# Expert rows loaded over the raw weights, summed, normed and multiplied tile by tile in one block

## What is computed

```python
for layer in range(2):
    h = rmsnorm(x, norm_mix[layer])
    ...
    x = x + mix                       # layer 1: mix = sgu_mixer(h, w_in [1024 x 4096], ...)
    x = x + memory_xattn(rmsnorm(x, norm_xattn[layer]), ...)
    x = x + moe_ffn(rmsnorm(x, norm_ffn[layer]), ...)   # 16 experts, top 2 for each position
```

## Time and profile before

| | |
|---|---|
| median of 3 runs | 1797.41 us (1796.53 to 1797.42) |
| profiled execution, its own time | 1796.38 us |
| its span, first to last instruction | 1794.6 us |
| instructions | 19043 |
| TensorE (PE) matmul busy | 84% of the span |
| VectorE (DVE), ScalarE (ACT), GpSimd (POOL) busy | 50%, 39%, 8% |
| granted TensorE clock, mean | 0.917 of full speed |
| HBM read and written | 267 and 25 MB |

### The profile page before, as it was taken

One profiled execution on the slowest core, in us unless ns is written; L12 is line 12 of the kernel. 1 busy time (PEld: TensorE's weight loads), 2 busy tenths in 40 slices (PEclk: granted clock), 3 DMA queues, 4 the chain that ended last, 5 costly groups with the idle time before them and its releaser, 6 DMA issues. The chain is left out here.

```text
span 1794.6 us, 19043 instructions
## 1 busy us (share of the span) xinstructions
PE 1514.5 (84%) x7481; PEld 1207.5 (67%) x7481; DVE 892.7 (50%) x1247; ACT 707.3 (39%) x1105; POOL 150.6 (8%) x172
## 2 busy tenths in 40 slices
PE   5689698879999893899995699797988894999992
PEld 4577566667777472888883588676877473888872
DVE  3156547575544525566653422743244435666653
ACT  3221355375333412555542333432133432555540
POOL 1000011200000000111101000503000000111110
PEclk9899789989999997899998799898999995999996
DMA  6523021023422053799983242213211133899964
GB/s 181 83 73 97 2 96 48 1 94 118 170 80 71 1 213 135 252 353 362 349 313 144 83 152 94 70 47 132 94 67 51 38 152 143 304 356 355 353 240 182
DMA packets 106874, 275.96 MB, mean 154 GB/s; under 512 B 37649, under 2 KB 40098, under 8 KB 101922
## 3 DMA queue, kind: packets, MB, share of 16 engines
q1 hardware_dynamic: 70818, 203.16, 32.1%
q10 hardware_dynamic: 26464, 54.79, 9.1%
q0 software_dynamic: 9504, 16.80, 2.5%
HBM read 267.31 MB, written 25.17 MB: 163 GB/s over the span
## 5 line engine op out<-in xcount | busy, mean ns | idle before, releaser
L185 DVE TENSOR_TENSOR w_lo<-w_stage,w_hi 128x2048 fp32r<-128x2048 f32 (+2 forms) x48 | 112.0, 2345 | 308.3 <-ACT w_hi L175 291.3
L175 ACT ACTIVATE w_hi<-w_stage 128x2048 fp32r<-128x2048 f32 (+2 forms) x48 | 86.4, 1812 | 338.1 <-PE bank L234 220.6
L2634 PE MATMUL bank<-e_wo,e_actT 128*128 128x512 f32 x384 | 170.4, 593 | 3.5 <-ACT e_actT L2696 3.5
L2517 DVE TENSOR_TENSOR e_wi_lo<-e_wi,w_hi 128x1536 fp32r<-128x1536 f32 x60 | 105.5, 1758 | 78.5 <-ACT w_hi L2513 78.5
L2634 PEld LDWEIGHTS bank<-e_wo,e_actT 128*128 128x128 f32 x384 | 72.2, 190 | 80.8 <-issue 78.9
L2513 ACT ACTIVATE w_hi<-e_wi 128x1536 fp32r<-128x1536 f32 x60 | 89.4, 1489 | 74.2 <-PE bank L2623 47.1
L2517 DVE TENSOR_TENSOR e_wi_lo<-e_wi,w_lo 128x1536 fp32r<-128x1536 f32 x60 | 105.5, 1758 | 16.5 <-ACT w_lo L2513 16.3
L2513 ACT ACTIVATE w_lo<-e_wi 128x1536 fp32r<-128x1536 f32 x60 | 89.0, 1483 | 17.2 <-PE bank L2623 17.2
L2623 PE MATMUL bank<-e_wi_lo,e_hx_hi 128*128 128x384 f32 x256 | 87.1, 340 | 0.0
L2622 PE MATMUL bank<-e_wi_lo,e_hx_hi 128*128 128x384 f32 x256 | 87.0, 340 | 0.0
L193 ACT ACTIVATE w_hi<-w_stage 128x2048 fp32r<-128x2048 f32 x26 | 49.6, 1912 | 85.1 <-PE bank L234 62.1
(11 more groups left out here) (490 smaller groups left out, 3840.9 us busy)
## 6 DMA issues: line engine op xcount, KB each, us to landing
e_wi<-in_moe_w_in SPq DMA_DIRECT2D x128, 768.0 KB, 6.0
e_wo<-in_moe_w_out ACTq DMA_DIRECT2D x30, 1536.0 KB, 9.4
w_stage<-in_x_wkv SPq DMA_DIRECT2D x16, 1024.0 KB, 5.2
w_stage<-in_sg_w_in SPq DMA_DIRECT2D x16, 1024.0 KB, 5.4
w_stage<-in_hyb_w_in SPq DMA_DIRECT2D x10, 1024.0 KB, 5.3
w_stage<-in_x_wq SPq DMA_DIRECT2D x8, 1024.0 KB, 5.0
w_stage<-in_x_wo SPq DMA_DIRECT2D x8, 1024.0 KB, 5.9
w_stage<-in_sg_w_out SPq DMA_DIRECT2D x8, 1024.0 KB, 5.0
```

The lines of the kernel that those rows point to most:

```text
L175: act.activation(self.w_hi[h][:, :, :cols], self.stage[h][:, :, :cols], ACT.Copy)\
L185: dve.tensor_tensor(self.w_lo[h][:, :, :cols], self.stage[h][:, :, :cols], self.w_hi[h][:, :, :cols], ALU.subtract).then_inc(self.lo_done[ ...
L2517: dve.tensor_tensor(self.lo[q][:, :, :], self.raw[q][:, :, :], self.hi[q], ALU.subtract).then_inc(self.wi_los[q], 1)
L2634: ins = pe.matmul(y_ps[n][:, :], auT[:, f, :], wo[j][:, f, n * GC:(n + 1) * GC], start=f == 0, stop=f == CO - 1)
```

## The change

What was the combine block and the norm block of layer 1 becomes part of the spatial-gating block; what was the last combine becomes part of the store block.

- The four buffers of raw weights and `wo0` become one tensor `room`, and the experts' 8 tiles of rows are loaded into its start. The loads are issued inside the experts' block, four by SyncE and four by ScalarE, each after a wait for the last scatter.
- The adds stand in a class `Combine`. The second add of a tile waits for the first; the first of the next tile waits for none.
- In layer 1, in one block: split of group 0, adds, norm by tiles (`NormTiles`, with the gain row), transposes to banks 0 to 3, their hi and lo parts, and the product of group 0 in the order given by hand, in banks 4 to 7. Even groups now use banks 4 to 7.
- The stores share a block with the last adds, each tile's store after its second add.
- The experts' weights for the sum (`wgt`) and the semaphores of the loads are allocated once for both layers.

```diff
     def product(self, pe, n, feature_major, banks, hi, lo, tiles=T, first=True, last=True, k0=0, halves=(0, 1),
-                ahead=None, tile_done=None):
+                ahead=None, tile_done=None, order=None):
...
+        order = order or [(h, b) for h in halves for b in range(n_tiles)]
+        left = [sum(h == i for h, _ in order) for i in range(2)]
+        begun = set()
+        for h, b in order:
+            if h not in begun:
+                begun.add(h)
+                pe.wait_ge(self.lo_done[h], n + 1)
+            if ahead is not None:
+                ahead(h, b)
...
+            left[h] -= 1
+            if left[h] == 0:
+                ins.then_inc(self.used[h], 1)

-def store_x(m, out):
+def store_x(m, combine, out):
     m.phase()
     stored = m.psem("x_stored")
+    combine.begin()
     with m.nc.Block() as block:
         @block.sync
         def _(sp):
             for t in range(T):
+                sp.wait_ge(combine.added, combine.ready(t))
                 sp.dma_start(out[0, t * P:(t + 1) * P, :], m.x[:, t, :]).then_inc(stored, 16)
             sp.wait_ge(stored, 16 * T)
+
+        @block.vector
+        def _(dve):
+            for t in range(T):
+                for c in range(2):
+                    combine.add(dve, t, c)

+class Combine:
+    ORDER = [c * T + i for i in range(T) for c in range(2)]
...
+    def load(self, engine, part):
+        for j in self.ORDER[part::2]:
+            engine.dma_start(self.y[:, j, :], self.y_dram[j * P:(j + 1) * P, :]).then_inc(self.m.y_in[j], 16)
...
+    def ready(self, t):
+        return 2 * (t + 1)
+
+    def add(self, dve, t, c):
+        m, j = self.m, c * T + t
+        dve.wait_ge(m.y_in[j], 16 * (self.layer + 1))
+        if c:
+            dve.wait_ge(self.added, 2 * t + 1)
+        dve.scalar_tensor_tensor(out=m.x[:, t, :], in0=self.y[:, j, :], scalar=m.wgt[:, j:j + 1],
+                                 in1=m.x[:, t, :], op0=ALU.mult, op1=ALU.add).then_inc(self.added, 1)

 def sgu_layer
...
-            norm_transpose(m, "mix1", m.x, a["norm_mix"][layer], T, hi, lo)
...
+            nt = NormTiles(m, "sg_n", c2, combine, v[:, :, D:SGW], junk[:, 0:D])
...
+            def bank(n):
+                return m.psum[4 * (1 - n % 2):4 * (1 - n % 2) + 4]
...
                 def _(sp):
+                    nt.load(sp, a["norm_mix"][layer])
                     sp.dma_start(ws[:, :, :], a["sg_ws"][0].rearrange("g t s -> t g s")).then_inc(ws_in, 16)
                     m.load(sp, first + NGR)
...
                 def _(pe):
+                    def turn(i):
+                        nt.turn(pe, i, [(lo_out, 2 * (i - 1))] if i >= 2 else [])
+
+                    def ahead(h, b):
+                        if h == 0:
+                            if b and b + 1 < T:
+                                turn(b + 1)
+                            pe.wait_ge(lo_out, 2 * (b + 1))
+
+                    turn(0)
+                    turn(1)
+                    m.product(pe, first, False, bank(0), hi, lo, ahead=ahead,
+                              order=[(0, 0), (1, 0), (0, 1), (1, 1), (0, 2), (0, 3), (1, 2), (1, 3)])
+                    for n in range(1, 2 * NGR):
...
                 def _(act):
...
                     m.split_hi(act, first)
+                    nt.square(act, 0)
+                    nt.take_root(act, 0)
+                    for i in range(1, T):
+                        nt.square(act, i)
+                        nt.take_root(act, i)
+                        keep_norm(i - 1)
+                    keep_norm(T - 1)
...
                 def _(dve):
...
+                    m.split_lo(dve, first)
+                    combine.add(dve, 0, 0)
+                    combine.add(dve, 0, 1)
+                    for i in range(T):
+                        if i + 1 < T:
+                            combine.add(dve, i + 1, 0)
+                        nt.normalize(dve, i)
+                        if i + 1 < T:
+                            combine.add(dve, i + 1, 1)
+                        if i:
+                            rest(i - 1)
+                    rest(T - 1)

 class Experts
...
-        self.raw = [m.sb(c, f"{nm}_wi{q}", [P, KC, 2 * DE]) for q in range(CI)]
+        room = m.sb(c, f"{nm}_room", [P, 2 * KD * DE + self.CO * D])
+        self.raw = [room[:, q * KC * 2 * DE:(q + 1) * KC * 2 * DE].rearrange("p (k n) -> p k n", k=KC) for q in range(CI)]
+        self.wo0 = room[:, 2 * KD * DE:].rearrange("p (f d) -> p f d", f=self.CO)
+        self.rows = room[:, 0:2 * T * D].rearrange("p (j d) -> p j d", d=D)
...
 def moe_experts
...
             def _(sp):
...
+                sp.wait_ge(stored[1], 16 * (NE // 2))
+                combine.load(sp, 0)
...
             def _(act):
...
+                act.wait_ge(stored[1], 16 * (NE // 2))
+                combine.load(act, 1)

-def moe_combine(m, layer, w, wgt, y_dram):
...
```

More of the change, by code:

```diff
@@ new lines, in product @@
+        n_tiles = -(-cols // P) if feature_major else tiles
+        order = order or [(h, b) for h in halves for b in range(n_tiles)]
[7 more added lines that the diff above has]
+                ahead(h, b)
+            for kk in range(KH):
+                k = k0 + KH * h + kk
+                for term, (x_part, w_part) in enumerate(((hi, self.w_hi[h]), (hi, self.w_lo[h]), (lo, self.w_hi[h]))):
+                    start = first and h == 0 and kk == 0 and term == 0
+                    stop = last and h == 1 and kk == KH - 1 and term == 2
+                    if feature_major:
+                        w_cols = slice(b * P, min(cols, (b + 1) * P))
+                        ins = pe.matmul(banks[b][:w_cols.stop - w_cols.start, :tiles * P], w_part[:, kk, w_cols],
+                                        x_part[:, k, :tiles * P], start=start, stop=stop)
+                    else:
+                        ins = pe.matmul(banks[b][:, :cols], x_part[:, k, b * P:(b + 1) * P],
+                                        w_part[:, kk, :cols], start=start, stop=stop)
+            if tile_done is not None and h == 1 and b < n_tiles - 1:
+                ins.then_inc(tile_done, 1)
+            left[h] -= 1
+            if left[h] == 0:
+                ins.then_inc(self.used[h], 1)
@@ L2046, in _, with sgu_layer @@
                 rest(XH - 1)
-def sgu_layer(m, layer, first, kv, cq):
+def sgu_layer(m, layer, first, kv, cq, combine):
     nc, a = m.nc, m.a
@@ L2086, in _ @@
                 def _(pool):
+                    nt.set_eps(pool)
                     pool.wait_ge(ws_in, 16)
@@ L2097, in _ @@
                 def _(pe):
-                    for n in range(2 * NGR):
+                    def turn(i):
[10 more added lines that the diff above has]
+                    for n in range(1, 2 * NGR):
                         if n >= 2:
                             pe.wait_ge(read, 4 * (n - 1))
-                        m.product(pe, first + n, n >= NGR, m.psum[4 * (n % 2):4 * (n % 2) + 4], hi, lo)
+                        m.product(pe, first + n, n >= NGR, bank(n), hi, lo)
                     pe.wait_ge(read, 4 * (2 * NGR - 1))
@@ L2891, in build_trunk @@
                 else:
-                    qT, kT, v = sgu_layer(m, layer, at["sgu"], kv, cq)
+                    qT, kT, v = sgu_layer(m, layer, at["sgu"], kv, cq, combine)
                 o_ctx = ExitStack()
@@ L2895, in build_trunk @@
                 cross_attend(m, f"x{layer}_at", qT, kT, v, *o, kv.back if layer else None)
-            moe(m, layer, at[f"xo{layer}"], o, o_ctx)
+            if layer == 0:
+                m.wgt = m.sb(ctx, "moe_wgt", [P, 2 * T])
+                m.y_in = [m.sem(f"y_in{j}") for j in range(2 * T)]
+            combine = moe(m, layer, at[f"xo{layer}"], o, o_ctx)
             if layer == 0:
                 right[0].close()
-        store_x(m, out)
+        store_x(m, combine, out)
 _INS = ["x", "mem", "positions", "norm_mix", "norm_xattn", "norm_mem", "norm_ffn", "hyb_w_in", "hyb_w_out",
```

69 lines of the change are left out of this document (31 added, 38 removed).

## The result

The changed kernel took **1786.74 us** (median of 6 runs, 1783.68 to 1791.24) against 1797.41 (6 runs, 1796.53 to 1797.86): a ratio of 0.9946, 95% interval 0.9932 to 0.9961. That is 10.7 us faster where I had forecast 18.8, and 1786.7 lies above the top of my range, 1784.5. The direction was right, the size was not.

What follows compares the result with a forecast made beforehand. TensorE is busy 84% of the span, so time is saved only where it stands still or is held back; 11.4 (part 2) plus 7.4 (part 3) gives 18.8 us less, forecast 1778.6 us, range 1775.5 to 1784.5.

Steps and rivals of the forecast that it cites:

- Part 1: Row loads at the experts' end: issued under POOL's 2.60 us DRAIN, next block still begins at about 975.5.
- Part 2: Layer 1's block from sum to product: group 0 ends 12.2 us earlier, less 0.8 for the mask, saving 11.4 us.
- The mask: POOL's mask of the gate's weights, now among the adds: costs 0.8 us, bounded by 0 and 2.2.
- The half-speed start stays ... as before: Start of the spatial-gating product: first matmuls at TensorE's half level lose 1.8 us, as in the queries stage.
- Other addresses in SBUF ... I cost at nothing: Whole kernel: tiles moved to other SBUF addresses by the change cost nothing.
- Behind it the product has no gap, so everything shifts: Rest of the product behind group 0: no gaps, so part 2's 11.4 us saving carries through whole.
- Part 3: Kernel end: earlier loads, and stores begun before the last add, save 7.4 us.
- rival 2: Kernel end: stores queue with loads, rows arrive late, last store is slow; saves 4.5 instead of 7.4 us; chance 0.14.
- its slow last store: Rival 2's claim at the kernel end: the last store takes 4.8 us to land, against 2.9 forecast.
- Of the rivals, 1: Block starts: POOL's DRAIN waits for the new loads, so blocks begin later; time 1795.9 us; chance 0.04.
- Rival 3: Interrupted product: TensorE's clock stays at half level through groups 0 and 1, 18 us slower, 1815; chance 0.02.
- its mild case: Rival 3 half way: a second half-speed stretch of 25 to 50 matmuls behind a wait, 1784 to 1789; chance 0.08.

Runs made afterwards that it cites:

- The kernel before with the pad alone: Kernel before the change with one extra 32-byte SBUF tensor a partition, open during layer 1's mixer, queries and attention: 1804.86 us (ratio 1.0046).
- the changed kernel with the pad taken back to 256: Changed kernel with 224 more bytes ahead of layer 1's tiles, making 256 with the change's 32: 1780.59 us (ratio 0.9906).
- the version with the mask, the clock and the held stores: Changed kernel, gate weights' load after the second weight group's, 12 and 22 dummy transposes before tiles 0 and 1's, stores held until all rows landed: 1783.69 us.

## Why the prediction was wrong in size

**Part 1 held.** Loads at the branch, a block start 3.0 us behind it, 2.60 us of DRAIN, the first add 6.36 us behind the start: each within 0.1.

**Part 2 held up to the first matmul and failed behind it.** Forecast 11.4, measured 9.6. The mask cost 0.4 instead of 0.8, and the first matmul came 0.3 us earlier than worked out; from it to the end of group 0 it took 27.2 us instead of 25.2. The step "The half-speed start stays ... as before" was mis-sized: I took 1.8 us from the queries stage, which by its trace comes from another state: TensorE is at the full level there until 3 us ahead of the product. Here it had been idle for 21 us at the half level, and 14 matmuls of the product ran so, where 6 had before: the first 24 with the transposes among them took 9.2 us where I had 8.0 (5.4, 1.8 and 0.8), so 1.2 more. It differs by program: 9.05 to 9.25 us in six profiles, 7.47 in one, and 6.36, 6.46 and 7.97 where TensorE had dummy work. Another 0.6 is the pace in group 0.

**"Other addresses in SBUF ... I cost at nothing" is the step that failed.** It cost 4.0 us in the rest of the product and 0.6 in group 0. Some 1.2 more, by the paces of its 192 matmuls (0.2332 for 0.2271), lie in x1_h, hidden in the -0.9 of the table. The kernel before with the pad alone shows it without the change, and the changed kernel with the pad taken back to 256 shows it undone: 1780.6 us, which is inside my range. In that kernel the branch to the end of group 0 took 49.0 us, 11.5 less than before where I had forecast 11.4, with 5 matmuls at the half level instead of 14. Between the spans it is 16.2 us below the kernel before: the rest of the 18.8 is 0.7 at the end, 1.1 in the product and gate, 0.8 ahead of layer 0's branch. "Behind it the product has no gap, so everything shifts" is true as written; a stretch without gaps can still be stretched by its pace. The rows of before held the warning: 0.2268 for h_sg and 0.2333 for um, the same instruction with the same shape at the same level. I read the pace of one product only and took it for the instruction's.

The Trainium skill, "TensorE: Matmul & The Clock Gate", section "Wait — 56ns, not 53.3ns?", gives 215.7 ns from start to start for 512 columns at the full level, and a fixed cost per matmul beside the columns. No row here agrees: 226.7 to 233.3 ns, and the part above the columns' 213.3 moves with the distance between two operands. The measurement decides.

**Part 3 held.** 6.7 against 7.4: the rows came 0.9 late, as rival 2 has it (it priced that at 1 us), but its slow last store did not come: 2.6 us, 0.3 quicker than I took and not 4.8.

**The rest of the table.** The +1.8 in layer 1 and the +1.7 ahead of layer 0's branch both lie in router and experts, and both go with the clock. In layer 1, over the stretch from 20 to 40 us into the stage, the granted clock was 0.64 to 0.66 in the changed kernel and 0.70 before; the version of 1780.6 us has 0.70 again, and 279.3 us. In layer 0 the last matmul of the attention's output came at 677.1 us (677.3 before), and from it to the branch it took 297.1 us (295.2 before); the clock over 20 us of it (712.7 to 732.7, and 712.9 to 732.9 before) was 0.63 and 0.68. The change is not what decides this: the kernel before with 64 bytes of pad, whose layer 0 is that of the kernel before, took 296.9 there, with 0.64, and the version with the mask, the clock and the held stores, whose layer 0 is that of the changed kernel, took 295.2, with 0.68. The changed kernel, run again, had 297.2 and 0.63. What decides between the two stays open.

Of the rivals, 1 did not happen. Rival 3, the clock, was right in kind and happened in its mildest form; its mild case, 25 matmuls or more at the half level, would have given 1784 to 1789, but there were 14. That 1786.7 lies in that band is chance: what put it there was mainly the price that I had named and left at nothing.

## What to carry to other kernels

Before a change that moves, adds or drops an allocation is costed, write down where each matmul's two SBUF operands begin. Read the pace of the same shape in several products; if it differs, hold their distance at a multiple of 256 bytes as part of the change, or a gain of 16 us may come out as one of 11. Costing by chains of instructions held to 0.3 us over 20 us; what it cannot see is the pace inside a full engine, so check one split-to-split interval of the untouched stretch behind a change first. In five versions a later stage of short bursts had more half-level time and took some 2 to 3 us more, and the stage of router and experts differed by 1.9 us between programs in which it was the same; so judge a version by its whole time, and a stage with the granted clock beside it.

## What the runs showed of the hardware

- A 512-column matmul at the full level starts 0.2267 us behind the last when the stationary tile and the streamed weights begin a multiple of 256 bytes apart in their partitions, 0.2289 at -64, and 0.2311 to 0.2333 at -64 with the weights as the stationary tile and at the other distances tried (+64, 128, +32, -32). It repeats run for run, and moving both by 32 bytes changes nothing.
- TensorE's level, once up, did not fall in waits of 1.4 us between dummy and real work in two kernels (first 24 matmuls in 6.36 and 6.46 us), and did in a third with the same instructions (8 matmuls at the half level, 7.97 us).
- A POOL mask of 1.09 us alone takes 1.75 beside two adds, and these 3.31 instead of 2.47.
- POOL's DRAIN behind the scatter is 2.60 us whether or not eight loads are in flight.
